# Kept rows leave from SP's queue block by block, three constants are loaded earlier, and the last attention's values use the output banks

## What is computed

```python
# hybrid_layer
x = x + 0.5 * swiglu_ffn(rmsnorm(x, ffn1_norm_g), ffn1_w_in, ffn1_w_out)
h = rmsnorm(x, mix_norm_g)
...
x = x + (g_nsa * o_nsa + g_conv * o_conv + g_mem * o_mem) @ w_out
x = x + 0.5 * swiglu_ffn(rmsnorm(x, ffn2_norm_g), ffn2_w_in, ffn2_w_out)
# second_block
h = _rms(x, norm_mix_w[l])
x = x + _mixer_block(h, ...)
x = x + _memory_xattn(_rms(x, norm_mem_q_w[l]), _rms(mem, norm_mem_kv_w[l]), ...)
x = x + _swiglu(_rms(x, norm_ffn_w[l]), ...)
return _rms(x, norm_final_w)
```

## Time and profile before

| | us |
|---|---|
| median of 3 runs | 2500.01 |
| lowest and highest | 2498.63, 3254.33 |
| the profiled execution | 2499.84 |
| its span, first to last instruction | 2498.0 |

### The profile page before, as it was taken

The page is one execution under the profiler, slowest core; times in us unless marked ns, Lnnn a source line. Parts: engine busy times, 40 slices in busy tenths (PEclk is TensorE's granted clock), DMA queues, the critical chain, the costliest instruction groups (busy, mean ns, idle before and its releaser), DMA issues.

```text
span 2498.0 us, 31231 instructions
## 1 busy us (share of the span) xinstructions
PE 2435.6 (98%) x11978; PEld 2032.0 (81%) x11978; DVE 1410.5 (56%) x2919; ACT 969.4 (39%) x1798; POOL 176.6 (7%) x244
## 2 busy tenths in 40 slices
PE   9999999999999999889999999999999998999997
PEld 7888888888887878778888888878878887888886
DVE  6435445676667666765443445667644566643444
ACT  4223234432345545653322334555423345422321
POOL 0000000101002211320000000222200002000000
PEclk9999999999999999999999999999999999999998
DMA  4454434333321122003223224211122432223222
GB/s 151 109 130 133 104 116 135 102 102 111 108 84 52 60 68 74 29 26 118 94 88 106 101 85 138 77 51 60 51 69 93 134 118 68 93 88 106 93 92 86
DMA packets 86381, 231.36 MB, mean 93 GB/s; under 512 B 8488, under 2 KB 23464, under 8 KB 86234
## 3 DMA queue, kind: packets, MB, share of 16 engines
q1 hardware_dynamic: 78768, 217.22, 26.8%
q10 hardware_dynamic: 7466, 12.14, 2.5%
HBM read 217.79 MB, written 11.53 MB: 92 GB/s over the span
## 4 chain that ended last, share of the span: by engine, by line
PE 91%; DVE 5%; ACT 3%; issue 1%; ACTq 0%; DMA 0%; POOL 0%; SPq 0%; DVEq 0%
PE bank L955 89%; PE bank L1148 2%; DVE t_PS L1843 0%; ACT t_PS L1441 0%; ACT t_pp L1580 0%; ACTq L1517 0%; DVE t_wlo L1838 0%; DVE t_pp L2072 0%; DVE t_QS L2165 0%; ACT t_whi L1441 0%; ACT t_tmp L1441 0%; PE bank L1322 0%; DMA t_XT<-in_xT 0%; DVE t_ST L2339 0%; DVE t_XT L2417 0%
## 5 line engine op out<-in xcount | busy, mean ns | idle before, releaser
L955 PE MATMUL bank<-t_XH,t_whi 128*128 128x512 f32 x2064 | 813.3, 394 | 5.9 <-DVE t_sa L2072 4.0
L955 PE MATMUL bank<-t_XH,t_wlo 128*128 128x512 f32 x2064 | 804.3, 390 | 0.0
L955 PE MATMUL bank<-t_XL,t_whi 128*128 128x512 f32 x2064 | 803.8, 389 | 0.0
L1838 DVE TENSOR_TENSOR t_wlo<-t_raw,t_whi 128x1024 fp32r<-128x1024 f32 (+2 forms) x418 | 479.5, 1149 | 373.7 <-ACT t_whi L1441 370.6
L1441 ACT ACTIVATE t_whi<-t_raw 128x1024 fp32r<-128x1024 f32 (+3 forms) x422 | 415.6, 988 | 418.9 <-PE bank L955 362.5
L955 PEld LDWEIGHTS bank<-t_XH,t_whi 128*128 128x128 f32 x2064 | 387.8, 188 | 89.6 <-DVE t_sa L2072 5.5
L955 PEld LDWEIGHTS bank<-t_XH,t_wlo 128*128 128x128 f32 x2064 | 387.5, 188 | 82.2
L955 PEld LDWEIGHTS bank<-t_XL,t_whi 128*128 128x128 f32 x2064 | 388.0, 188 | 77.3
L955 PE MATMUL bank<-t_RX,t_whi 128*128 128x512 f32 x1056 | 325.1, 389 | 0.0
L1942 DVE TENSOR_TENSOR t_tmp<-bank,t_RB 128x512 f32<-128x512 f32 x178 | 122.5, 688 | 227.2 <-PE bank L955 222.2
L955 PEld LDWEIGHTS bank<-t_RX,t_whi 128*128 128x128 f32 x1056 | 198.2, 188 | 41.2
(11 more groups left out here) (313 smaller groups left out, 2748.6 us busy)
## 6 DMA issues: line engine op xcount, KB each, us to landing
t_raw<-in_f_in SPq DMA_DIRECT2D x86, 512.0 KB, 3.2
t_raw<-in_f_out SPq DMA_DIRECT2D x32, 384.0 KB, 3.1
t_raw<-in_w_conv SPq DMA_DIRECT2D x24, 512.0 KB, 3.2
t_raw<-in_w_merge SPq DMA_DIRECT2D x24, 512.0 KB, 3.2
t_raw<-in_fg SPq DMA_DIRECT2D x22, 512.0 KB, 3.2
t_raw<-in_fu SPq DMA_DIRECT2D x22, 512.0 KB, 3.2
t_raw<-in_f_out SPq DMA_DIRECT2D x32, 320.0 KB, 2.8
t_raw<-in_w_g SPq DMA_DIRECT2D x16, 512.0 KB, 3.2
```

The costliest lines, as they stand in the source:

```text
L955: return e.matmul(o, l, r, start=start, stop=stop, skip_group_check=True)
L1838: e.tensor_tensor(wlo[n % NRAW][:, 0:width], raw[n % NRAW][:, 0:width], f32(whi[n % NHI][:, 0:width]), ALU.subtract).then_inc(*w_lo.tick(n))
```

## The change

- `spill` moves from ACT's program to SP's, and from the end of the feed-forward block into its last loop: after the `norm` of each output block m, SP waits for `("xt", i, m)` and issues that block's DMA.
- ACT's part of `winzero` becomes an item of its own, `winload`, that stands in the second feed-forward block, after output block 0 of the first half. DVE's part stays where it was.
- In `memory2` the rings are set to `HEADA` before `mv2`; `mv2` takes banks of the role "ov"; `mq2s` 1 moves from before tile 3 to before tile 5 (tile 1 of head 1).

```diff
@@ ffn
                 if h:
                     norm(nxt, m)
+                    if f < 2:
+                        w.add("spill", f, m)
+                elif f == 1 and m == 0:
+                    w.add("winload")
@@ memory2
         w.lin("mq2", 0, name="w_mq2", j=0)
         w.add("nstat", 4)
+        w.add("banks", HEADA)
         w.lin("mv2", 0, name="w_mv2", j=0)
@@
-        at = [{2: lambda: w.lin("mv2", 1, name="w_mv2", j=1), 3: both(one("mv2s"), one("mq2s", 1))}, {}, {}, {}]
+        at = [{2: lambda: w.lin("mv2", 1, name="w_mv2", j=1), 3: one("mv2s")}, {1: one("mq2s", 1)}, {}, {}]
         after = [{}, dict(after=first_out), {}, dict(after=one("om", 1))]
-        w.add("banks", HEADA)
@@
     ffn(0, 0, "f1_in", "f1_in", "f1_out", 0, 2 * KF, 1, [Job(mem_norm(0))])
-    w.add("spill", 0)
@@
     ffn(1, 2, "f2_in", "f2_in", "f2_out", 0, 2 * KF, 3, [])
-    w.add("spill", 1)
@@ pe_program, mv2
-            natural([("mv2", i) for i in range(2)], n, j, 2, *MX2, ("m", 1), 256, 4)
+            natural([("mv2", i) for i in range(2)], n, j, 2, *MX2, ("m", 1), 256, 4, "ov")
@@ act_program
-        def spill(i):
-            for k in range(KD):
-                on.wait_ge(*evac.at(("xt", (1, 3)[i], k)))
-                e.dma_start(xs[k * P:(k + 1) * P, :], XT[:, k, :]).then_inc(*d_s[k].tick(i, by=16))
@@
-        def winzero():
+        def winload():
             on.wait_ge(*full.at(("ffo", 1, 0, 0)))
             e.dma_start(mask, A["mask"]).then_inc(*d_mask.tick(0, by=16))
@@ sp_program
+        def spill(i, k):
+            on.wait_ge(*evac.at(("xt", (1, 3)[i], k)))
+            e.dma_start(xs[k * P:(k + 1) * P, :], XT[:, k, :]).then_inc(*d_s[k].tick(i, by=16))
```

More of the change, by code:

```diff
@@ L1816, in act_program @@
         e.dma_start(vec, A["vec"]).then_inc(*d_vec.tick(0, by=16))
-        do = dict(start=start, relload=relload, norm=norm, normsq=normsq, memload=memload, memnorm=memnorm, ffg=ffg, spill=spill, convg=convg,
+        do = dict(start=start, relload=relload, norm=norm, normsq=normsq, memload=memload, memnorm=memnorm, ffg=ffg, convg=convg,
                   wide=wide, widefin=widefin, memvs=memvs, mgate=mgate, sgate=sgate,
@@ L1820, in act_program @@
                   sqfin=sqfin, sk=sk, skfin=skfin, skput=skput, svs=svs, cclear=cclear, cscore=cscore, csoft=csoft, cturn=cturn,
-                  msplit=msplit, winzero=winzero, kaz=kaz, vas=vas, qa=qa, oa=oa, om=om, gdec=gdec, gexp=gexp, gln=gln, gcum=gcum, gvt=gvt,
+                  msplit=msplit, winload=winload, kaz=kaz, vas=vas, qa=qa, oa=oa, om=om, gdec=gdec, gexp=gexp, gln=gln, gcum=gcum, gvt=gvt,
                   gsq=gsq, gg=gg, osplit=osplit, mk2d=mk2d, mv2s=mv2s, mq2s=mq2s)
@@ L2525, in sp_program @@
         n = 2
-        do = dict(table=table, msplit=msplit, final=final)
+        do = dict(spill=spill, table=table, msplit=msplit, final=final)
         for (kind, *args), upto in w.items:
```

## The result

The changed kernel takes 2494.24 us (median of 12 runs, 2492.78 to 2499.46), the kernel before 2500.24 us (median of 12). The ratio is 0.9978, with a 95% interval of 0.9971 to 0.9985: 0.2% faster, and within 2%. One execution of the kernel before (3254.33 us) and one of experiment E3 (11497.92 us) stand far off all others; they count in the medians and not in the ratios. The profiled execution has a span of 2492.4 us against 2498.0.

The account below looks back on a forecast made before the run. The prediction took PE to bound the kernel, busy 2435.6 of 2498.0 us. 3.0 + 1.5 + 0.9 + 0.5 = 5.9 us off 2499.84 gave 2493.9, said as 2494, range 2492.5 to 2495.5, or 2491.2 to 2497.8 with rivals.

Parts of the forecast that it names:

- First mixer, 3.0 + 1.5 us: First mixer's start: 3.0 us of PE idle time goes, and 1.5 us of lowered clock behind it returns.
- second term: First mixer's third unit: full-speed work lost to the clock drop behind PE's stall returns, 1.5 us.
- Second mixer, 0.9 us: Second mixer's start: PE's wait for the root goes once ACT's six issues are moved, 0.9 us.
- The moved steps at nothing: Output blocks: kept blocks in SP's queue and the three constants on ACT cost PE nothing.
- The cover of 5 us per load: SP's loads beside the output blocks: each can come about 5 us later before PE has to wait.
- Rival 1: SP's queue: kept blocks hold up the loads, deciding above 0.37 us per block; 21 us slower, 2515; chance 5%.
- first two terms: First mixer's start: 3.0 us of PE idle time and 1.5 us of clock behind it.
- Attention over memory, 0.5 us: Attention over memory: bank wait of 2.36 us goes, about 4.1 us idle opens before tile 5; gain 0.5 us.
- Rival 3: Attention over memory: new idle time keeps the clock at 1.2 GHz, costing 1.5 us instead of gaining 0.5; 2496; chance 12%.
- Rival 4: Attention over memory: removing the bank wait gains its full 2.36 us plus 0.5 of clock; 2491.5; chance 8%.
- The sum, 5.9 us: Whole kernel: both mixers and the attention over memory together take 5.9 us off, giving 2494 us.
- the range: Whole kernel: forecast's own range 2492.5 to 2495.5 us, 2491.2 to 2497.8 with rivals 2 to 4 added in part.

Follow-up runs that it names:

- E3: Changed kernel with the kept blocks issued by ACT instead of SP, still block by block: 2495.62 us, ratio 0.9977 to the kernel before.
- E4: Changed kernel with all eight kept blocks issued behind the feed-forward block, still by SP: 2495.59 us, ratio 0.9981 to the kernel before.
- E9: Kernel before with only the kept blocks moved, block by block in SP's queue: 2495.25 us, ratio 0.9981 to the kernel before.
- E5: Changed kernel with the kept blocks back in ACT's queue behind the feed-forward blocks; constants' loads and memory part stay: 2500.44 us, one run.
- E2: Kernel before with the memory part of the change alone: 2500.01 us, ratio 0.9996 to the kernel before.
- E12: Kernel before, unchanged, run and profiled once more: 2498.81 us, one run.
- E1: Changed kernel with the memory part taken back: 2493.96 us, ratio 0.9977 to the kernel before.
- E8: Changed kernel with `nstat` 4 in one of the first six banks and the values' second half moved before tile 5: 2494.94 us, ratio 0.9980.

## Why the prediction was right

**First mixer, 3.0 + 1.5 us: right, 0.24 us too small.** The steps came as told: split at 372.67 (predicted 372.5), low part, statistic, root by 377.1 (predicted about 377), no idle time, a clock of 1.00. The stretch fell by 4.74 us. The small miss is in the second term: 0.43 x 4 = 1.72 us of clock was cut by 0.2 us for the time in which PE was idle, and 3.03 + 1.72 = 4.75 is what came. It looks as if the clock was still full until PE resumed, but no row shows that. Against other executions of the old placement (13.87, 13.31, 14.02 us) the gain is 3.7 to 4.4 us: the issues' length and the clock behind the stall vary. E3, E4 and E9 show the cause: every way of taking the issues from in front of the split gives 9.63 or 9.64 us, and leaving them there (E5) 14.02.

**Second mixer, 0.9 us: right in this pair of profiles, wrong as a property of the kernel.** The split comes at 1531.11, 5.51 us behind the last add, which is the predicted 1536 in the times of the kernel before; but it does not stand right behind ACT's square, as it waits 2.58 us for PE to free its buffer. The step that failed is to read a wait of 0.86 us in one execution as if each had it. It ended a chain of nine DMA issues whose length moved by 0.9 us between executions (the split at 1537.47 in E2 is 7.25 us behind the last add, in the kernel before 8.13 us). A second profile of the kernel before gives 0.08 us to gain.

**The moved steps at nothing: right.** PE stays at 60.00 of 60 us, the issues last 0.33 us each on SP (0.72 to 0.97 on ACT before), and the landing falls from 4.4 to 3.1 us. The cover of 5 us per load was given without its working. Rival 1 was given its deciding point in microseconds per block, which was of little use, since blocks cost PE nothing at six times the traffic (share 0.84) and did at ten, where the DMA engines and SP's queue are both full. The advice of the Trainium skill (Perfetto Trace Analysis, DMA Optimizations) to keep inputs and outputs on different engines makes no difference here: E3 follows it and E9 does not, at 9.64 us each. The Trainium skill (DMA: Bandwidth & Descriptors, Issuing engines are not separate DMA queues) calls an issue's time "usually small relative to the DMA itself". The trace agrees: 0.97 us against 5.7 us to the landing for the blocks at the first mixer before, 0.33 against 3.1 in the changed kernel. The prediction left out the last words when it set the sentence against its first two terms. Small beside the transfer does not mean small for PE: in front of a split that PE waits for, eight issues cost 4 us of 2500.

**Attention over memory, 0.5 us: the new wait right, the gain 0.2 us or nothing.** The new idle time is 4.03 us (about 4.1 predicted), ended by `mq2s` as told; POOL's run is broken after two tiles, and the end comes 0.65 us earlier (28.30 to 27.65), though only 0.34 us earlier than in E12 (27.99). What failed is the step that costs the bank move by the scores alone: I followed who takes which bank after `mv2`, and not who had just used banks 6 and 7. `nstat` 4 had; PE waits for DVE to read it, and the stretch is 0.41 us longer. E1, E2 and E8 agree on that to 0.01 us. Rival 3's condition came: a clock of 0.64 and 0.51 between 2084 and 2092 us, which is 1.2 GHz for nearly all of the second window, with PE busy for 4.00 us of 4 there. Its price did not: PE still comes early enough to wait 0.47 us for POOL at 2098.05 and 0.75 us for DVE at 2099.21. Rival 4 fell as well, and E8 shows it from the other side: PE's idle time there can be filled without gaining anything.

**The sum, 5.9 us: 5.6 in the profile and 6.0 in the medians, in part by cancelling.** What the change does, over all profiles at hand: 3.7 to 4.7 us at the first mixer, 0.1 to 1.0 at the second, -0.2 to 0.3 in the attention, together 3.6 to 6.1. The rest of the profile's difference is clock (-1.49 at 1853 us, 0.8 at the end), -0.4 us ahead of the first mixer and 0.6 us between the mixers, whose stretch takes 1145.2 to 1149.1 us in the profiles with up to six writes and 1145.7 to 1145.8 in the kernel before. Where I looked, the idle times in it are the same and the clock behind them differs (at 768 us it falls to 0.68 in E9 behind 2.39 us of idle time, and stays at 1.00 in the changed kernel behind the same). I had not put this scatter of 1 to 3 us into the range; the median hit its middle. E3 shows how far one execution can be off: over its runs its ratio (0.9977) is that of the changed kernel (0.9978), and yet its profiled execution took 2497.61 us, with 3.2 us more between the mixers.

## What to carry to other kernels

A DMA issue is cheap or dear by what the DMA engines are doing at that moment, so look for rows of issues at a change of stage, where the next stage's loads already fill the engines, and ask which compute instruction stands behind them on the issuing engine. Spread the issues over a stretch with idle DMA engines, or give them to an engine for which nothing waits: each alone is enough. Before a role gets other buffers, list who used those buffers last as well as who will use them next; and profile the old kernel twice before a wait under 1 us enters a sum.

## What the hardware showed that I had not expected

**An issue's length follows the load of the DMA engines, on either queue.** Median of a block's issue beside output blocks: 0.33 us on SP and on ACT with one write (share 0.43 to 0.47), and for the further copies 0.38 us with three writes (0.64), 0.47 us with six (0.84) and 0.57 us with ten (1.03 where they run). Behind the feed-forward block it is 0.57 to 0.61 us, and the longest last 1.19 to 1.55 us on ACT. The share alone does not set it: at a share of about 1.0 behind the first feed-forward block an issue takes 0.65 us on SP in E4 (mean of eight) and 0.84 to 0.97 us on ACT in E2, E5, E12 and the kernel before (mean of the last six).

**The clock behind an idle time of 0.9 to 2.4 us is not fixed.** Behind the same 2.04 us it stayed at full speed in one of 14 profiles and fell in the others, at a price of 1.5 us. Two executions of the changed kernel took the same course at each of these places, two of the kernel before did not, and kernels that differ only elsewhere took others. What decides stays open.
